# Attention stage of a three-layer transformer kernel: value tokens first, query chunks between the pairs

## The reference, cut to what matters

```python
proj = h @ w_in[l]
qa, ka, va, qb, ckv, qi, ki, wi = jnp.split(proj, offsets, axis=-1)
out_a = dilated_mixture(qa, ka, va, slopes_a)            # 8 heads of 64
ckv = rmsnorm_2(ckv, kv_norm_g[l])
q_lat = einsum('bthd,hdr->bthr', qb, w_uk[l])            # 8 latent heads
o_lat = sparse_attention(qi, ki, wi * IDX_SCALE, q_lat, ckv, slopes_b)   # top 128 keys of each query
out_b = einsum('bthr,hrd->bthd', o_lat, w_uv[l])
x = x + ga1 * (concat([out_a, out_b]) @ w_out[l])
```

## Time and profile before

| | |
|---|---|
| median of the timed runs | 2023.68 us |
| profiled execution, its own time | 2021.82 us |
| span of the trace | 2020.0 us |
| TensorE busy | 1947.8 us, 96% |
| VectorE, ScalarE, GpSimd busy | 1048.7, 447.2, 1183.6 us |
| mean granted TensorE clock | 0.983 |

### The profile page before, as it was taken

The page is one execution under the profiler, slowest core; times in us unless marked ns, Lnnn a source line. Parts: engine busy times, 40 slices in busy tenths (PEclk is TensorE's granted clock), DMA queues, the critical chain, the costliest instruction groups (busy, mean ns, idle before and its releaser), DMA issues.

```text
span 2020.0 us, 25249 instructions
## 1 busy us (share of the span) xinstructions
PE 1947.8 (96%) x8772; PEld 1563.7 (77%) x8772; DVE 1048.7 (52%) x1588; ACT 447.2 (22%) x762; POOL 1183.6 (59%) x907
## 2 busy tenths in 40 slices
PE   7999999999999999998999999999997899999998
PEld 6787868888888877655888888886775588888886
DVE  5566257766646353557666663234857563232222
ACT  3302342112110022432221111012116421111100
POOL 3653325878877956223688787743550157666673
PEclk7999999999999999998999999999999999999999
DMA  7432223555555422111355553321210023232232
GB/s 298 167 125 73 94 94 104 188 187 203 188 200 179 156 91 83 42 42 46 133 201 193 194 188 127 104 95 63 84 63 22 11 84 104 93 101 97 95 113 73
DMA packets 67518, 242.25 MB, mean 120 GB/s; under 512 B 7642, under 2 KB 8026, under 8 KB 67458
## 3 DMA queue, kind: packets, MB, share of 16 engines
q1 hardware_dynamic: 65536, 237.01, 34.2%
q10 hardware_dynamic: 1922, 4.40, 0.6%
HBM read 239.28 MB, written 2.10 MB: 119 GB/s over the span
## 4 chain that ended last, share of the span: by engine, by line
PE 89%; DVE 4%; ACT 3%; issue 2%; DMA 1%; POOL 1%; SPq 0%; DVEq 0%; ACTq 0%; POOLq 0%
PE gemm L443 24%; PE gemm L445 23%; PE gemm L444 23%; PE gemm L470 2%; PE gemm L472 2%; PE gemm L471 2%; DMA w_raw<-wstream 1%; PE mix L646 1%; PE mix L443 1%; PE gemm L799 1%; PE mix L444 1%; PE mix L445 1%; PE mix L952 1%; PE gemm L813 1%; PE mix L554 1%
## 5 line engine op out<-in xcount | busy, mean ns | idle before, releaser
L427 POOL TENSOR_TENSOR w_lo<-w_raw,w_hi 128x1024 fp32r<-128x1024 f32 x302 | 741.1, 2454 | 25.2
L443 PE MATMUL gemm<-h_hi,w_hi 128*128 128x512 f32 x1616 | 635.4, 393 | 14.3 <-DVE h_lo L1123 6.4
L444 PE MATMUL gemm<-h_lo,w_hi 128*128 128x512 f32 x1616 | 631.1, 391 | 0.0
L445 PE MATMUL gemm<-h_hi,w_lo 128*128 128x512 f32 x1616 | 631.0, 390 | 0.0
L424 POOL TENSOR_TENSOR pool_gate<-pool_gate 128x1 f32<-128x1 f32 x298 | 104.2, 350 | 764.6 <-PE gemm L445 619.7
L443 PEld LDWEIGHTS gemm<-h_hi,w_hi 128*128 128x128 f32 x1616 | 305.0, 189 | 83.9 <-issue 13.4
L425 POOL TENSOR_SCALAR w_hi<-w_raw 128x1024 fp32r<-128x1024 f32 x302 | 351.1, 1163 | 18.4 <-DMA w_raw<-wstream 18.4
L445 PEld LDWEIGHTS gemm<-h_hi,w_lo 128*128 128x128 f32 x1616 | 304.7, 189 | 64.0
L444 PEld LDWEIGHTS gemm<-h_lo,w_hi 128*128 128x128 f32 x1616 | 305.2, 189 | 62.7
L1017 DVE CUSTOM_DVE_ANT_0 ada_raw<-ada_raw,c_act 128x1024 f32<-128x1024 f32 x128 | 219.4, 1730 | 106.2 <-DMA ada_raw<-adastream 106.2
L445 PE MATMUL gemm<-p_hi,w_lo 128*128 128x512 f32 x528 | 205.4, 389 | 0.0
(11 more groups left out here) (323 smaller groups left out, 1999.9 us busy)
## 6 DMA issues: line engine op xcount, KB each, us to landing
w_raw<-wstream SPq DMA_DIRECT2D x302, 512.0 KB, 3.5
ada_raw<-adastream SPq DMA_DIRECT2D x128, 512.0 KB, 4.3
a_early<-adastream SPq DMA_DIRECT2D x8, 1024.0 KB, 13.2
out<-x_res SPq DMA_DIRECT2D x8, 256.0 KB, 2.2
x_res<-x_in SPq DMA_DIRECT2D x2, 512.0 KB, 6.4
c_act<-c_in ACTq DMA_DIRECT2D x2, 512.0 KB, 7.2
x_res<-x_in ACTq DMA_DIRECT2D x2, 512.0 KB, 9.0
b_dist<-const_in ACTq DMA_DIRECT2D x1, 512.0 KB
```

Source lines behind the costliest of these rows:

```text
L427: pool.tensor_tensor(wlo[s][:], raw[:, u % RAW, :], whi[s][:].bitcast(F32), ALU.subtract).then_inc(w_split, 1)
L443: pe.matmul(out_ap, w_h, r_h, start=first, stop=False)
L444: pe.matmul(out_ap, w_h, r_l, start=False, stop=False)
L445: return pe.matmul(out_ap, w_l, r_h, start=False, stop=last)
```

## The change

The order of the weight stream and of the queues in the attention stage is changed.

- The four value chunks come first, the q and k chunks follow pair by pair (q0, k0, q1, k1, ...). Four tile chunks stand before the latent keys and values and four behind.
- The scores of pair 0 are issued right behind the latent values; the other four q and k chunks, the scores of pair 1 and one query chunk of the latent heads follow, then the loop.
- The other three query chunks are cut into slices of 2, 2, 2, 1 and 1 k steps (`query_part`), between the turned pieces of pairs 0, 1 and 2. They accumulate in bank `gemm1`, so turned pieces 0 to 19 all use bank `gemm0` and each waits for the copy of the one before. From piece 20 on two banks alternate again.
- `h_hi` is read until the last query chunk is done. So the outputs of pairs 0 and 1 are kept in tiles 10 and 11 of `T2`, whose queries are used up by then, and their high parts are made together with pair 2's, their low parts in VectorE's round 3.
- ScalarE empties a query chunk behind the five copies of its pair (`evict(13 + p, ...)`), ahead of `exps(2p + 3)`.

```diff
@@ -917,15 +917,16 @@
...
             mm.then_inc(norm_sum, 1)
-            def attn_tiles(first):
-
-                for u in range(4):
-                    tile_chunk(N0["attn_in"] + first + u, (N0["attn_in"] + u) % SPL, u, G0["attn_in"][u] + first // 4)
-
-            attn_tiles(0)
+            def attn_tile(c, bank, use):
+
+                n = N0["attn_in"] + c
+                tile_chunk(n, n % SPL, bank, G0["attn_in"][bank] + use)
+
+            token_body(N0["attn_in"], N0["attn_in"], list(G0["attn_in"]))
             bc[0] += 1
             bcast(rstdps, bc[0])
-            attn_tiles(4)
+            for u in range(4):
+                attn_tile(4 + u, u, 1)
@@ -933,15 +934,14 @@
...
                 pe.matmul(M[j][:], T2[:, 5, j * P:(j + 1) * P], wuv[:], start=True, stop=True).then_inc(sig("vb_mm"), 1)
-            token_body(N0["attn_in"] + 8, N0["attn_in"] + 8, [g + 2 for g in G0["attn_in"]])
...
                 else:
-                    if p == 4:
-                        pe.wait_ge(gfree[1], G0["attn_out"][1])
+                    if p >= 4:
+                        pe.wait_ge(gfree[1], G0["attn_in"][1] + 3 + p - 3)
                     pe.wait_ge(sig("att_z"), 2 * p)
@@ -956,25 +956,45 @@
...
-            def turn(p, pieces):
-
-                for c in pieces:
-                    n = 5 * p + c
-                    pe.wait_ge(sig("att_p"), 2 * p + (1 if c < 2 else 2))
-                    if n < 2:
-                        pe.wait_ge(gfree[n], G0["attn_out"][n])
-                    else:
-                        pe.wait_ge(sig("att_c"), n - 1)
-                    for a, i, o in PIECES[c]:
-                        z = Z[(2 * p + a) % 4]
-                        for j in range(i, NTB):
-                            mm = pe.transpose(G[n % 2][:, o + P * (j - i):o + P * (j - i) + P],
-                                              z[:, OFF_J[j] + i * P:OFF_J[j] + (i + 1) * P], const("ident"))
-                    mm.then_inc(sig("att_t"), 1)
+            def turn_bank(n):
+
+                return G[0] if n < 20 else G[n % 2]
+
+            def turn(p, c):
+
+                n = 5 * p + c
+                pe.wait_ge(sig("att_p"), 2 * p + (1 if c < 2 else 2))
+                if n == 0:
+                    pe.wait_ge(gfree[0], G0["attn_out"][0])
+                elif n <= 20:
+                    pe.wait_ge(sig("att_c"), n)
+                else:
+                    pe.wait_ge(sig("att_c"), n - 1)
+                for a, i, o in PIECES[c]:
+                    z = Z[(2 * p + a) % 4]
+                    for j in range(i, NTB):
+                        mm = pe.transpose(turn_bank(n)[:, o + P * (j - i):o + P * (j - i) + P],
+                                          z[:, OFF_J[j] + i * P:OFF_J[j] + (i + 1) * P], const("ident"))
+                mm.then_inc(sig("att_t"), 1)
+
+            def query_part(u, first, count):
+
+                n = N0["attn_in"] + 12 + u
+                s = n % SPL
+                if first == 0:
+                    pe.wait_ge(w_split, n + 1)
+                    pe.wait_ge(gfree[1], G0["attn_in"][1] + 3 + u)
+                for k in range(first, first + count):
+                    mm = three(G[1][:], whi[s][:, k * P:(k + 1) * P], wlo[s][:, k * P:(k + 1) * P],
+                               Hhi[:, k, :], Hlo[:, k, :], k == 0, k == KT - 1)
+                if first + count == KT:
+                    mm.then_inc(pe_done, 1)
...
                     pe.wait_ge(gfree[2], G0["attn_out"][2])
+                elif p < 3:
+                    pe.wait_ge(sig("att_kept"), p)
                 else:
@@ -988,16 +1008,29 @@
...
             scores(0)
-            for u in range(2):
-                tile_chunk(N0["attn_in"] + 12 + u, (N0["attn_in"] + u) % SPL, u, G0["attn_in"][u] + 3)
+            for u, (bank, use) in enumerate(((0, 2), (1, 2), (2, 2), (0, 3))):
+                attn_tile(8 + u, bank, use)
             scores(1)
-            for u in range(2):
-                tile_chunk(N0["attn_in"] + 14 + u, (N0["attn_in"] + 2 + u) % SPL, u, G0["attn_in"][u] + 4)
+            query_part(0, 0, KT)
             for p in range(8):
-                turn(p, (0, 1))
+                parts = p < 3
+                turn(p, 0)
+                if parts:
+                    query_part(p + 1, 0, 2)
+                turn(p, 1)
+                if parts:
+                    query_part(p + 1, 2, 2)
                 if p + 2 < 8:
                     scores(p + 2)
-                turn(p, (2, 3, 4))
+                turn(p, 2)
+                if parts:
+                    query_part(p + 1, 4, 2)
+                turn(p, 3)
+                if parts:
+                    query_part(p + 1, 6, 1)
+                turn(p, 4)
+                if parts:
+                    query_part(p + 1, 7, 1)
                 values(p)
@@ -1597,7 +1630,8 @@
...
                 dve.wait_ge(hhi_ready, KT * 7 + k + 1)
-                dve.tensor_tensor(Hlo[:, k, :], G[2][:], Hhi[:, k, :].bitcast(F32), ALU.subtract).then_inc(h_ready, 1)
+                src = T2[:, 10 + k, :] if k < 2 else G[2][:]
+                dve.tensor_tensor(Hlo[:, k, :], src, Hhi[:, k, :].bitcast(F32), ALU.subtract).then_inc(h_ready, 1)
@@ -1611,7 +1645,10 @@
...
                     bias(2 * p + 5)
-                if p >= 1:
+                if p == 3:
+                    pair_low(0)
+                    pair_low(1)
+                if p >= 3:
                     pair_low(p - 1)
@@ -1973,19 +2010,23 @@
...
-            for u in range(4):
-                evict(u, u, 10 + u, 0.125)
-            for u in range(4):
-                evict(4 + u, u, 14 + u)
+            act.wait_ge(pe_done, N0["attn_in"] + 4)
+            for j in range(4):
+                act.activation(VA[:, j, :], G[j][:], ACT.Copy).then_inc(gfree[j], 1)
+            evict(4, 0, 10, 0.125)
+            evict(5, 1, 14)
+            evict(6, 2, 11, 0.125)
+            evict(7, 3, 15)
             for u in range(4):
...
                 act.activation(VB[:, j, :], M[j][:], ACT.Copy).then_inc(sig("vb_copied"), 1)
-            act.wait_ge(pe_done, N0["attn_in"] + 12)
-            for j in range(4):
-                act.activation(VA[:, j, :], G[j][:], ACT.Copy).then_inc(gfree[j], 1)
+            evict(8, 0, 12, 0.125)
+            evict(9, 1, 16)
+            evict(10, 2, 13, 0.125)
+            evict(11, 0, 17)
@@ -2001,27 +2042,37 @@
...
                     n = 5 * p + c
+                    bank = G[0] if n < 20 else G[n % 2]
                     act.wait_ge(sig("att_t"), n + 1)
...
                         dst = PS[:, c // 2, 512 * (c % 2):512 * (c % 2) + 512]
-                        ins = act.activation(dst, G[n % 2][:], ACT.Copy)
+                        ins = act.activation(dst, bank[:], ACT.Copy)
                     else:
-                        ins = act.activation(PS[:, :, 1024:TRI], G[n % 2][:].rearrange("p (a t) -> p a t", a=2), ACT.Copy)
+                        ins = act.activation(PS[:, :, 1024:TRI], bank[:].rearrange("p (a t) -> p a t", a=2), ACT.Copy)
                     ins.then_inc(sig("att_c"), 1)
...
                 act.wait_ge(sig("att_o1"), k + 1)
+                if k < 2:
+                    act.activation(T2[:, 10 + k, :], G[2][:], ACT.Copy).then_inc(sig("att_kept"), 1)
+                    return
+                if k == 2:
+                    act.wait_ge(pe_done, N0["attn_in"] + 16)
+                    act.wait_ge(sig("att_kept"), 2)
+                    for early_pair in range(2):
+                        act.activation(Hhi[:, early_pair, :], T2[:, 10 + early_pair, :], ACT.Copy).then_inc(hhi_ready, 1)
                 act.activation(Hhi[:, k, :], G[2][:], ACT.Copy).then_inc(hhi_ready, 1)
...
             exps(1)
-            for u in range(4):
-                evict(12 + u, u % 2, 6 + u, 0.125)
+            evict(12, 1, 6, 0.125)
             for p in range(8):
...
                 copy_turned(p)
+                if p < 3:
+                    evict(13 + p, 1, 7 + p, 0.125)
                 if p + 1 < 8:
@@ -2067,11 +2118,12 @@
...
     heads = [a[:, 128 * h:128 * h + 128] for h in range(4) for a in (qb, kb)]
+    pairs = [a[:, 128 * h:128 * h + 128] for h in range(4) for a in (b_qa, b_ka)]
     chunks = [tile_chunks(np.concatenate([qa, fa], 1)), token_chunks(ia), tile_chunks(ga), token_chunks(vb), tile_chunks(np.concatenate(heads, 1)),
...
               tile_chunks(i["odd_w_out"][0]), tile_chunks(pair_tiles(i["ffn_w_in"][1])), down_chunks(i["ffn_w_out"][1]),
-              tile_chunks(np.concatenate([qi, ki, ki, ckv, b_qa, b_ka], 1)), token_chunks(b_va), tile_chunks(b_qb),
+              tile_chunks(np.concatenate([qi, ki, ki, ckv], 1)), token_chunks(b_va), tile_chunks(np.concatenate(pairs, 1)), tile_chunks(b_qb),
               tile_chunks(i["w_out_2"][0]), tile_chunks(pair_tiles(i["w_gu_2"][0])), down_chunks(i["w_down_2"][0])]
...
     assert wstream.shape[0] == NCHUNK
```

(2 more changed lines are left out.)

## The result

The changed kernel took 2030.22 us (median of 8 runs, 2025.86 to 2032.73), the kernel before 2023.58 on the same chip (8 runs, 2022.21 to 2026.18): a ratio of 1.0032, interval 1.0022 to 1.0042. It is slower by 6.6 us. I had forecast 2024.6 and no change; the time lies outside my range and almost on rival 2's 2030.3. A later series of the same two kernels gave 1.0030 (1.0016 to 1.0043), a difference of 5.6 us.

What follows compares the result with a forecast made beforehand. TensorE, 89% of the chain, was taken as the bound, within its stretch 1410 to 1561 us. A 0.6 us gain by scores 6 and a 1.5 us clock fall made +0.9: 2024.6 from median 2023.68, range 2018.5 to 2029.

Steps and rivals of the forecast that it cites:

- rival 2: Slower: a clock fall follows each stall of 2.5, 1.95, 1.95 and 4.3 us; +6.6 us, 2030.3, chance 0.22.
- Start: Up to pair 0's first turn: scores 0 at 1464.15, scores 1 from 1488.4, first turn 1496.3 instead of 1515.81.
- the wait at the swap: TensorE at value chunk 4, which needs bank 0 copied out: 0.15 us lost, bounds 0 and 0.95.
- the early scores start nothing: Pair 0's exponentials stand behind four evictions and a table load on ScalarE, so exponential 0 runs only from 1490.5.
- GpSimd's splits: Splits behind three chunks ending in the loop may block VectorE: priced at 0, or 1.5 us in three rounds.
- The clock: TensorE's granted clock falls once, at pair 3's stall of 4.3 us: 1.5 us added.
- Rounds: From one pair's values start (V) to the next: 15.3 us, TensorE standing 1.95 at turn 1, against 10.54 plus 5.44.
- rival 1: Faster: turn 1's wait is covered, TensorE's 13.0 to 13.3 us sets the round, no fall; -7.0 us, 2016.7, chance 0.2.
- Part switches at 0: Switches between query slice and turn on TensorE cost 0 to 0.2 us, fifteen times, 0 to 3; taken as 0.
- Pair 3: Single bank with nothing to fill it: TensorE stands 4.3 us at turn 1, scores 6 at V + 19.65 = 1560.5.
- the same work: From scores 6 on, both kernels have the same work and two banks, so no difference was counted there.
- its turning point: The slower case decides from the third clock fall on, at +4.7 us.

Runs made afterwards that it cites:

- e8: Changed kernel, but ScalarE makes exponentials 0 and 1 ahead of the last tile chunk's eviction: 2023.05 us, ratio 1.0002 to the kernel before.
- e1: Changed kernel, but query chunk 12 is reported to GpSimd only within pair 2's scores, so its split starts some 8 us later: 2026.48 us, ratio 1.0019.
- e3: Changed kernel, but ScalarE copies the first turned piece of pairs 0 to 3 ahead of exponentials 2p+2: 2020.46 us, ratio 0.9991 to the kernel before.
- e6: Changed kernel with first turned piece copied ahead of exponentials in pairs 0 to 3 and the split behind chunk 12 later: 2016.28 us, ratio 0.9964.
- e7: Changed kernel with first piece copied ahead in pairs 0 to 2, chunk 12's split later, two banks from piece 15 on: 2017.11 us, ratio 0.9960.
- e5: Kernel before, but turned pieces 0 to 19 all use bank gemm0 and wait for the previous piece's copy: 2045.22 us, ratio 1.0110.

## Why the prediction was wrong

Taken step by step, with 4.1 us off the times of after:

- *Start.* Forecast scores 0 at 1464.15, scores 1 at 1488.4, first turn 1496.3; measured 1464.1, 1488.5, 1496.5. Scores 0 came within 0.1 us, so the wait at the swap was not priced too low, and "the early scores start nothing" held: exponential 0 at 1490.5, as forecast. e8 shows that the order in ScalarE's queue was the reason.
- *GpSimd's splits: "I price it at 0".* **This step failed: a term put at nothing that measured 2.1 us.** I looked at the three chunks that end inside the loop, at V + 1.3 to V + 3.7, and found VectorE with time to spare. The split behind chunk 12 I did not place at all. By my own times it was w_lo from about 1497.6 to 1500.0 (chunk end at 1496.3, then the 1.3 from gate to w_lo of the earlier trace rows), and group 2's negation was due at about 1498.2, on the chain to exponential 2, the copy and turn 1. Cost 2.1 us, shown by e1. The range I gave for the lock, up to 1.5, was for the wrong place.
- *The clock: "I add one".* **This failed too: the one of 1.5 us came, and two more besides, of 2.5 and 1.6.** Turn 1 of pair 3 drew its fall as forecast. But pair 0's stall had become 4.30 us through the lock and drew one, worth 2.5 us to the start of the values (11.56 against e1's 9.08), and a fall came at scores 6 as well, worth 1.6 by the end of the stage. The falls at 1488 and 1539 before went out of the sum as gained, with one to replace them; three came.
- *Rounds.* 15.3 forecast, 15.08 and 15.09 measured, -0.4 in all; the stall 1.68 against 1.95. The order in ScalarE's queue, on which rival 1 turned, decided as I said, and e3 shows what it is worth.
- *Part switches at 0, of a bound of 3.* Right: in rounds 0 and 1 no gap but the stall at turn 1 shows on TensorE.
- *Pair 3.* Stall 4.09 against 4.3. Scores 6 at V + 21.24 against 19.65 + 1.5 for the fall: as forecast within 0.1.

**The sum again, to the start of scores 6.** Forecast -0.6 + 1.5 = +0.9. With 2.1 for the lock, 2.5 for the fall in pair 0 and -0.4 for the rounds it is +5.1. Measured: 1570.47 - 4.1 = 1566.37 against 1561.09, +5.28. From scores 6 to the last values, where I had "the same work", it is 35.44 us against 33.88, another +1.56: the clock falls at scores 6 (0.58 in the last window of after) and did not there before. The two make the 6.8 us of the stage. That these sums close is in part built in, since 2.1 and 2.5 were read from e1 against the same trace of after; the medians alone bear out no more than the total.

**Rival 2 had the time and not its terms.** It put a fall of 1.5 to 1.9 us behind each of four stalls. Measured, the two stalls of 1.68 us passed at 1.00, and 2.1 us of the loss was no clock at all, so that its time is right by luck. A third fall came, as its turning point asked, but at scores 6 and behind none of its four stalls. Rival 1's rounds of 13 to 13.3 us are nearly what e3 and e6 reach (13.6), and e6's 2016.3 is close to its 2016.7; both are other kernels, in which the wait that rival 1 took as covered was taken away.

What stays open: why the clock fell at scores 6 in after, behind a 1.94 us wait that e3, e6 and e7 also have there and pass at 1.00. It fell in both profiles of after and in neither e1 nor e8, which differ from it only ahead of pair 0's values. In these two the fall behind the last long wait, 2.47 us at turn 0 of pair 6, is missing too, and every other trace has it. I also can't say why e6 gains 4.8 us over e3 in the medians. The stage is 2.7 us shorter in the profiles, and 1.6 of that is e3's longer first fall, ahead of the edits; that leaves the 1.2 us of the wait for VectorE. They ran on different chips, and the difference of the medians is uncertain by some 3 us.

## What to carry to other kernels

Where a helper engine's long operation follows a TensorE chunk, lay its start and end beside every small operation on the critical chain, at each place where it now occurs, and not only where the pattern repeats. Before giving up a second buffer, look at what stands ahead of the copy that frees the first: here moving one copy a pair ahead of a group's exponentials was worth 9 us, give or take 3, and left the single bank nearly free. List the falls of the clock of the kernel before as a term of its own, with the longest stalls of the new one against it: they neither cancel nor stay where they were. And take a second profile of both kernels before a fall is counted, for executions of one kernel differ by as much as a fall costs.

## What the runs showed of the hardware that I had not expected

- A VectorE operation on 128x4 elements, 0.17 us alone, took 2.26 us (2.31 in e3) when it started 0.1 us behind a GpSimd operation of 2.4 us, and 0.17 us again when e1 moved that operation away.
- The falls of the granted clock came again at the same instructions in two profiles each: 8.5 and 8.5 us of (1 - clock) before, 11.9 and 11.9 after. Still, behind the same wait of 2.5 us in pair 6 ten traces have a fall and two (e1, e8) have none.
- Filling 3.6 us of each of the two long stalls (0.70 and 0.46 us of them were left) kept the clock at 1.00 there; two falls came elsewhere, and the median gained 0.7 us.
- With one bank, serial turns and copies and a stall of 2.9 us a round, the sum of (1 - clock) in e5 doubled (17.1 against 8.5), and a change with an estimated 10 us of added waits cost 20.5.
